# Forgetting-attention scores over 65 rows in place of 128, without the clearing of the key pads

## What is computed

```
s = jnp.einsum('bqhd,bkhd->bhqk', q, k).astype(jnp.float32) * (HD_B ** -0.5)
s = s + (jnp.swapaxes(c_q, 1, 2)[..., :, None] - jnp.swapaxes(c_k, 1, 2)[..., None, :])
s = jnp.where((pos_k[None, :] <= pos_q[:, None])[None, None], s, -jnp.inf)
p = jax.nn.softmax(s, axis=-1).astype(v.dtype)
return jnp.einsum('bhqk,bkhd->bqhd', p, v)
```

## Time and profile before

| | |
|---|---|
| median of 3 runs | 2351.91 us (2348.36 to 2354.6) |
| the profiled execution's own time | 2352.33 us |
| its span, first to last instruction | 2350.5 us |
| PE busy, share of the span | 2117.8 us, 90% |
| DVE busy | 1465.4 us, 62% |
| ACT busy | 702.3 us, 30% |
| GpSimd busy | 265.5 us, 11% |
| mean granted TensorE clock | 0.945 of full speed |

### The profile page before, as it was taken

How to read it: one execution, slowest core, us unless ns; L and a number is a source line. 1 busy time by engine, 2 the same in 40 slices (tenths; PEclk the granted TensorE clock), 3 DMA queues, 4 the chain that set the end, 5 groups by cost and what they waited for, 6 DMA issues and landing times. The chain is left out here.

```text
span 2350.5 us, 27654 instructions
## 1 busy us (share of the span) xinstructions
PE 2117.8 (90%) x10002; PEld 1258.5 (54%) x10002; DVE 1465.4 (62%) x3175; ACT 702.3 (30%) x1536; POOL 265.5 (11%) x364
## 2 busy tenths in 40 slices
PE   3999999989978999988869999998999699999797
PEld 3534465555436777744444344655544477777343
DVE  3369489987986645422134685999979866454222
ACT  3351233332112233333234503333311222333231
POOL 0000233231000000001100003233210000000011
PEclk9999999999986799989979999999999858999899
DMA  8201222213220003023351112312141200220332
GB/s 276 75 23 70 84 85 90 94 44 102 67 70 17 5 24 117 14 87 121 116 176 54 57 50 68 120 60 88 46 130 38 70 12 8 82 70 1 107 142 94
DMA packets 151112, 179.40 MB, mean 76 GB/s; under 512 B 71312, under 2 KB 106640, under 8 KB 150704
## 3 DMA queue, kind: packets, MB, share of 16 engines
q1 hardware_dynamic: 122912, 140.23, 18.8%
q10 hardware_dynamic: 28064, 37.38, 4.5%
HBM read 120.25 MB, written 67.22 MB: 80 GB/s over the span
## 5 line engine op out<-in xcount | busy, mean ns | idle before, releaser
L850 PE MATMUL ps<-wring,xnT_arena 128*128 128x512 f32 (+2 forms) x2304 | 920.3, 542 | 0.0
L850 PEld LDWEIGHTS ps<-wring,xnT_arena 128*128 128x128 f32 x2304 | 404.2, 191 | 354.0 <-issue 337.3
L1600 DVE TENSOR_SCALAR_CACHE_REDUCE arena<-arena,theta 32x1056 bf16<-32x1056 f32 x496 | 459.9, 979 | 2.2
L1187 PE MATMUL ps<-wring,arena 128*128 128x512 f32 x576 | 257.7, 607 | 0.0
L1264 ACT COPY arena<-ps 128x512 f32<-128x512 f32 (+3 forms) x144 | 75.3, 523 | 448.8 <-PE ps L850 415.1
L1815 DVE TENSOR_REDUCE small<-ps 128x1 f32<-128x192 f32 (+9 forms) x148 | 114.0, 771 | 142.9 <-PE ps L1121 140.7
L1187 PEld LDWEIGHTS ps<-wring,arena 128*128 128x128 f32 x576 | 111.9, 197 | 134.9 <-issue 134.9
L1483 ACT ACTIVATE arena<-ps,small 128x192 f32<-128x192 f32 (+9 forms) x148 | 111.1, 751 | 216.2 <-DVE small L1815 215.8
L1119 PE MATMUL ps<-xnT_arena,arena 128*128 128x64 f32 (+4 forms) x336 | 124.5, 503 | 20.2 <-DVE xnT_arena L1229 19.1
L2016 POOL TENSOR_TENSOR arena<-arena 128x1024 f32<-128x1024 f32 x16 | 37.5, 2345 | 901.3 <-DVE arena L1843 901.3
L986 PEld LDWEIGHTS ps<-arena 128*128 128x128 f32 x488 | 69.5, 193 | 107.4 <-DVE arena L1707 78.9
(11 more groups left out here) (245 smaller groups left out, 2558.4 us busy)
## 6 DMA issues: line engine op xcount, KB each, us to landing
projected<-arena ACTq DMA_DIRECT2D x130, 256.0 KB, 2.0
arena<-residual SPq DMA_DIRECT2D x36, 512.0 KB, 5.2
wring<-in_w_in SPq DMA_DIRECT2D x16, 1024.0 KB, 7.7
o_bc<-projected SPq DMA_DIRECT2D x36, 384.0 KB, 3.7
wring<-in_w_in SPq DMA_DIRECT2D x6, 2048.0 KB, 8.8
arena<-projected SPq DMA_DIRECT2D x18, 512.0 KB, 5.2
residual<-arena SPq DMA_DIRECT2D x18, 512.0 KB, 2.6
wring<-in_w_out SPq DMA_DIRECT2D x8, 1024.0 KB, 6.4
```

The lines of the kernel that those rows point to most:

```text
L850: o = mm(bank(pbank(k), 0, w_), xnT[:, c, t * P:(t + 1) * P], w, start=(c == 0), stop=(c == CH - 1))
L1187: o = mm(bank(4 - 4 * (t % 2) + half), yT[t % 2][:, c, :], wring[:, c * D + 512 * half:c * D + 512 * half + 512], start=(c == 0), stop=(c ...
L1600: V.tensor_scalar(cmp_out[r, (i % 2) * WMAX:(i % 2) * WMAX + uw[u]], score[u][r], th_, 0.0, op, ALU.add, accum_out=into[r, i:i + 1]).then_ ...
```

## The change

The fox scores take slices of 65 rows of `QT` and `foxKT`; the dsa scores keep 128. The two clearings at L1778 and L2001 go, and with them the semaphore and its four waits. In place of its wait for the pads ACT gets a wait for the last projection matmul, since its copies also write over `xnT`. GpSimd's own wait for that matmul goes.

```
-        pad_keys, pad_rest = sem("pad_keys"), sem("pad_rest")
+        pad_rest = sem("pad_rest")
...
                         if n == 0:
-                            pe.wait_ge(pad_keys, 2)
                             pe.wait_ge(pad_rest, 1)
...
-                        qt = QT[unit_no[mu] % 4]
-                        kt = foxKT if m == "fox" else dsaKT["s" if u == "s" else "p"][:, None, :]
+                        rows = HD + 1 if m == "fox" else P
+                        qt = QT[unit_no[mu] % 4][0:rows]
+                        kt = foxKT[0:rows] if m == "fox" else dsaKT["s" if u == "s" else "p"][:, None, :]
...
-                    act.wait_ge(pad_keys, 2)
+                    act.wait_ge(p_mm, p_mm_at[jobs[-1]])
                     act.wait_ge(pad_rest, 1)
...
                     dve.wait_ge(p_mm, p_mm_at[jobs[-1]])
-                    V.memset(foxKT[HALF:, 0:2], 0.0).then_inc(pad_keys, 1)
...
-                    dve.wait_ge(pad_keys, 2)
                     for what, key in PLAN:
...
                         if n == NKA:
-                            pool.wait_ge(p_mm, p_mm_at[jobs[-1]])
                             pool.wait_ge(ka_ready, ka_ready_at[FKS[NKA - 1]])
-                            nc.gpsimd.memset(foxKT[HALF:, 2:4], 0.0).then_inc(pad_keys, 1)
-                            pool.wait_ge(pad_keys, 2)
```

## The result

The changed kernel took 2391.49 us (median of 4 runs, 2387.57 to 2393.68) against 2352.47 us for the kernel before (4 runs). The ratio is 1.0166 with a 95% interval of 1.0146 to 1.0186: 39 us slower, where 3.8 us less had been forecast. Its profiled execution has a span of 2390.6 us, 40.1 us above the one of before.

The account below looks back on a forecast made before the run. The prediction took DVE's clearing at the start of the attention stage to bound the kernel; 2 x 1.90 us gave 3.8 us less and zero for the 65-row passes, so 2348.1 us, range 2336 to 2357.

Parts of the forecast that it names:

- What bounds the kernel now: Start of the attention stage: DVE's clearing at L1778 lies whole on the chain, 1.88 us; GpSimd's clearing is hidden.
- 2 x 1.90 us = 3.8 us less: Attention start, each layer: without DVE's clearing the first key copy starts 1.90 us earlier, at 684.65 rather than 686.55.
- I take zero for each pass: Fox score passes on PE: contracting over 65 rows instead of 128 saves next to nothing, so zero was counted.
- the sum: Whole kernel: 2 x 1.90 us = 3.8 us less, 0.16%, with zero for the 65-row passes.
- PE's clock falls more: Rival, fox part: one more half-clock stretch of 20.5 us per layer, 6.6 to 14.4 us slower; chance 0.05 for the upper half.
- so there is more to lose than to gain: Argument for the faster-clock rival (0.36): the fox part is at half clock for nearly half of its 150 us.
- The array is set up anew for 65 rows: Rival, fox scores alternating with 128-row mask matmuls: 0.21 us per entry, 28.6 us in all, time 2377; chance 0.08.
- The four times shown lie within 6.2 us: Argument against the faster-clock rival (0.36): the kernel's run times suggest its clock pattern is rather steady for one program.

Follow-up runs that it names:

- clear_65: The kernel before with both clearings and all waits kept, only the fox scores' contraction cut to 65 rows; 2399.91 us, ratio 1.0205.
- no_clear_128: The changed kernel with the fox scores' contraction put back to 128 rows and nothing cleared; 2343.18 us, ratio 0.9957 to the kernel before.
- fill_one: no_clear_128 plus one matmul of a zero stationary over 128 rows per fox prompt job (two in the widest unit); 2341.89 us, ratio 0.9956.
- fill_one_65: fill_one with the added zero matmuls contracting over 65 rows in place of 128; 2365.47 us, ratio 1.0056 to the kernel before.
- fill_two: no_clear_128 with twice as many added zero-stationary matmuls over 128 rows as fill_one; 2337.32 us, ratio 0.9944 to the kernel before.

## Why the prediction was wrong

- *"What bounds the kernel now"* held. The clearing of DVE lay on the chain, GpSimd's was hidden, and ACT's and GpSimd's earlier work moved no end by itself.
- *"2 x 1.90 us = 3.8 us less"* was mis-sized. The copy came 2.36 us closer to the search, since the idle time ahead of L1778, which was to stay, fell from 0.59 us to 0.13. And the first row maximum came closer to the last step of the search by 4.3 us (12.58 before, 696.47 less 683.89; 8.30 after), because PE's clock rose ahead of the sample scores. Between medians the clearing is worth 8 to 9 us (clear_65 against the change, the kernel before against no_clear_128); only a part of that is traced to a place.
- *"I take zero for each pass"* is the step that failed. It was right for the pass at a given clock, and wrong as the price of the cut. The step asked only what a pass over 65 rows takes at a given clock, which is the same within 5 ns. It did not ask what it does to the clock. no_clear_128 against the change (2343.18 and 2391.49 us), and fill_one against fill_one_65 (2341.89 and 2365.47), show that fewer rows bring the clock down by themselves: 48 us where the sum had zero.
- The rival *"PE's clock falls more"* was the right mechanism in the wrong size and for the wrong reason. It thought of the earlier start as the cause, allowed one more stretch of 20.5 us per layer, and gave it 0.05. Measured, the fox parts have some 54 to 61 us more at half clock in each layer than the kernel before. Its price, 0.16 to 0.35 us per us, was good: 0.33.
- *"so there is more to lose than to gain"* read the half-clock stretches as a reserve. They were the sign of a stage near the edge, from which it could be pushed further down. They were also less of it than was said: the fox part lasted 178.3 us and not 150, and 68 us are 38% of it, not nearly half.
- *"The array is set up anew for 65 rows"* did not happen. The Trainium skill's page TensorEngine Tiling (Array Packing), under Available Configurations, has no mode between 64 and 128 rows, and the trace agrees: 4.8 us of idle time ahead of the mask loads against 4.3. With 64 rows it happens, at 0.37 us a time.
- *"The four times shown lie within 6.2 us"* was too few runs to call the pattern steady. With 35 runs in the last comparison the kernel before spread from 2341.25 to 2362.63.

## What to carry over

Zero rows of a matmul take no time, but they can hold the clock up. Before cutting a contraction, look at the granted clock of that stage. If it changes between 1.0 and 0.5 there, price the cut by us at half clock (here 0.33 us for each) and not by the pass; a stage at a steady 1.0 is no proof of a margin, as the sparse part showed. To drop the clearing of a pad, leave the contraction as it is and let the pad of one operand hold finite leftovers where the other's is zero; that is no_clear_128, 0.4% faster than the kernel before. With two fillers per job it is 0.6% (fill_two), not told apart from it. A start that moves by 2 us was worth more than its length here; how much more can't be read from one profiled execution, since the clock's pattern differs between executions and between the layers of one.

## What the runs showed of the hardware

- The clock follows the rows that a matmul contracts over: the mean in the fox part goes 0.55 to 0.58, 0.67, 0.70 to 0.75, 0.81 and 0.78 to 0.85 for 64, 65, 96, 112 and 128 rows.
- The values don't have to matter for that. Rows of zeros on both sides (the kernel before, 0.80) and leftovers against zeros (0.85 and 0.78) keep the clock up alike, and so does a stationary of nothing but zeros (0.89 and 0.88).
- A busy engine can stay at half clock: in the changed kernel PE was at 0.50 for 129.7 us on end in the first layer, busy for 127.3 of them.
- Going between matmuls over 64 rows and over 128 rows costs a pause, 0.21 us at the full clock and 0.37 where the clock is mostly half. Over 65, 96 and 112 rows there is none to be seen (ahead of the mask loads of the first layer 4.8, 4.7 and 4.1 us in all, against 4.3 with 128).
- Runs of one kernel spread by 0.9% (2341.25 to 2362.63 us in 35) where the forecast took 0.3% for what can be told.
